# ScalarE's table sets named in the code: one set for Ln and Exp in each norm, the Silu set ahead of each feed-forward loop

## What is computed

```python
def rmsnorm(x, g):
    y = x * lax.rsqrt(jnp.mean(x * x, axis=-1, keepdims=True) + EPS)
    return y * g

def conv_ffn(h, w_gate, w_up, conv, w_down):
    u = dwconv3(h @ w_gate, conv)              # three taps along the tokens
    return (jax.nn.silu(u) * (h @ w_up)) @ w_down

for layer in range(DEPTH):
    mod = jax.nn.silu(cond) @ w_ada[layer] + b_ada[layer]
    shift1, scale1, gate1, shift2, scale2, gate2 = jnp.split(mod, 6)
    h = rmsnorm(x, norm_mix_g[layer]) * (1 + scale1) + shift1
    y = mixer_ab(h, ...) if layer % 2 == 0 else multiscale_pool(h, ...)
    x = x + gate1 * y
    h = rmsnorm(x, norm_ffn_g[layer]) * (1 + scale2) + shift2
    x = x + gate2 * conv_ffn(h, ...)
y = rmsnorm(x, final_norm_g)
```

## Time and profile before

| | |
|---|---|
| three runs | 1548.97, 1555.16, 1557.83 us |
| profiled execution | 1552.02 us, its span 1550.2 us |
| mean granted TensorE clock | 0.965 |
| TensorE matmul | 1417.5 us busy, 91% |
| VectorE | 1007.2 us, 65% |
| GpSimd | 670.3 us, 43% |
| ScalarE | 408.5 us, 26%, 50 table loads among its 718 instructions |
| DMA | 163.2 MB, mean 105 GB/s |

### The profile page before, as it was taken

How to read it: one execution, slowest core, us unless ns; L and a number is a source line. 1 busy time by engine, 2 the same in 40 slices (tenths; PEclk the granted TensorE clock), 3 DMA queues, 4 the chain that set the end, 5 groups by cost and what they waited for, 6 DMA issues and landing times.

```text
span 1550.2 us, 24701 instructions
## 1 busy us (share of the span) xinstructions
PE 1417.5 (91%) x9517; PEld 1376.2 (89%) x9517; DVE 1007.2 (65%) x1377; ACT 408.5 (26%) x718; POOL 670.3 (43%) x400
## 2 busy tenths in 40 slices
PE   3799979889979799999999999886999999999995
PEld 1598969888969699999999999875999999999995
DVE  4795688988666577787878887345664155325654
ACT  4723322155440633201110111256331011001122
POOL 0263544400515265565656554311454545454542
PEclk9899989999989899999999999987999999999998
DMA  9242312163123133443334442210332222222222
GB/s 380 101 136 96 100 37 69 55 227 116 50 71 122 68 122 135 171 148 135 122 116 169 144 140 76 74 41 14 122 108 82 68 82 68 71 78 81 66 72 79
DMA packets 44790, 163.23 MB, mean 105 GB/s; under 512 B 4800, under 2 KB 5952, under 8 KB 43584
## 3 DMA queue, kind: packets, MB, share of 16 engines
q1 hardware_dynamic: 44736, 162.52, 30.3%
HBM read 154.12 MB, written 6.82 MB: 104 GB/s over the span
## 4 chain that ended last, share of the span: by engine, by line
PE 69%; DVE 18%; issue 6%; ACT 5%; DMA 1%; ACTq 0%; POOL 0%; DVEq 0%; SPq 0%; POOLq 0%
PE ps L675 58%; DVE ada_raw L1454 3%; DVE work L1471 2%; DVE junk L1454 2%; DVE work L1477 2%; PE ps L960 2%; DVE work L1468 1%; ACT work L1029 1%; DVE blocks L1647 1%; PE ps L687 1%; DVE outer L1644 1%; DVE work L1847 1%; ACT work L1160 1%; ACT work L1360 1%; DVE qkv L1573 1%
## 5 line engine op out<-in xcount | busy, mean ns | idle before, releaser
L599 POOL TENSOR_SCALAR whi<-raw 128x1024 fp32r<-128x1024 f32 (+1 forms) x172 | 193.7, 1126 | 736.0 <-PE ps L675 567.8
L675 PE MATMUL ps<-hhi,whi 128*128 128x320 f32 x1984 | 461.5, 314 | 46.7 <-DVE hlo L1438 30.1
L675 PE MATMUL ps<-hlo,whi 128*128 128x320 f32 x1984 | 455.4, 311 | 0.0
L675 PE MATMUL ps<-hhi,wlo 128*128 128x320 f32 x1984 | 455.3, 311 | 0.0
L602 POOL TENSOR_TENSOR wlo<-raw,whi 128x1024 fp32r<-128x1024 f32 (+1 forms) x172 | 442.3, 2572 | 14.4
L675 PEld LDWEIGHTS ps<-hhi,whi 128*128 128x128 f32 x1984 | 335.4, 190 | 56.2 <-issue 32.6
L675 PEld LDWEIGHTS ps<-hlo,whi 128*128 128x128 f32 x1984 | 335.7, 190 | 0.0
L675 PEld LDWEIGHTS ps<-hhi,wlo 128*128 128x128 f32 x1984 | 335.3, 190 | 0.0
L675 PE MATMUL ps<-hidhi,whi 128*128 128x320 f32 x704 | 161.0, 310 | 2.8 <-DVE hidlo L1850 2.8
L675 PE MATMUL ps<-hidhi,wlo 128*128 128x320 f32 x704 | 161.0, 310 | 0.0
L675 PE MATMUL ps<-hidlo,whi 128*128 128x320 f32 x704 | 161.0, 310 | 0.0
(11 more groups left out here) (203 smaller groups left out, 1267.5 us busy)
## 6 DMA issues: line engine op xcount, KB each, us to landing
raw<-in_w_gu SPq DMA_DIRECT2D x88, 512.0 KB, 3.2
ada_raw<-in_w_rows SPq DMA_DIRECT2D x70, 512.0 KB, 3.5
raw<-in_w_in SPq DMA_DIRECT2D x28, 512.0 KB, 3.3
raw<-in_w_dn SPq DMA_DIRECT2D x32, 448.0 KB, 3.3
ada_first<-in_w_ada SPq DMA_DIRECT2D x4, 2048.0 KB, 21.6
raw<-in_w_dn SPq DMA_DIRECT2D x16, 512.0 KB, 3.3
row_late<-in_w_rows SPq DMA_DIRECT2D x10, 512.0 KB, 3.3
raw<-in_w_out SPq DMA_DIRECT2D x8, 512.0 KB, 4.1
```

The lines of the kernel that those rows point to most:

```text
L599: nc.gpsimd.tensor_scalar(whi[s][:, 0:n], raw[s][:, 0:n], 1.0, 0.0, ALU.mult, ALU.add).then_inc(s_whi, 1)
L675: last = nc.tensor.matmul(pair[pr][:, b], wt[s][:, cs], act[:, k, b * HALF:(b + 1) * HALF], start=(j == 0 and q == 0), stop=(j == len(tile ...
```

## The change

The warm-up Ln in `rsqrt_of_sums` and the one ahead of the scan output's norm are replaced by an explicit load of the set that holds both Ln and Exp. Ahead of the groups of each layer's feed-forward, behind the modulation, the Silu set is loaded by name. The activations, the waits and all other engines' streams stay as they are.

```diff
--- before.py
+++ after.py
@@ -45,6 +45,7 @@
 ADA_FFN = 48
 GROUPS = [8, 7, 7]
 EPS = 1e-6
+LN_EXP, SILU = "natural_log_exp_and_others", "silu_and_others"
 TILES = [S0 + P * t for t in range(SEQ_S // P)] + [P0]
 NT = len(TILES)
 BLOCK = 32
@@ -1006,7 +1007,7 @@
 
 
                 own.sync()
-                own.tick(nc.scalar.activation(warm[:], eps_col, ACT.Ln))
+                nc.scalar.preload_act_table_set(LN_EXP)
                 act.wait_ge(s_norm, q + 1)
                 if q:
                     act.wait_ge(s_a, 8 * q)
@@ -1292,8 +1293,7 @@
                 for n, (_, s_done) in enumerate(done_visits):
                     if s_done == s - 1:
                         o_squares(n)
-            own.sync()
-            own.tick(nc.scalar.activation(warm[:], eps_col, ACT.Ln))
+            nc.scalar.preload_act_table_set(LN_EXP)
             o_squares(NT - 1)
             own.sync()
             own.tick(nc.scalar.activation(ssq[:, 1], ssq[:, 0], ACT.Ln, bias=eps_col, scale=1.0 / DK))
@@ -1348,6 +1348,7 @@
                         mix_squares(g - 1)
                     mix_squares(3)
                     modulate(3, 1, 1)
+                nc.scalar.preload_act_table_set(SILU)
                 for g, nf in enumerate(GROUPS):
                     b = SEG["up", layer, g]
                     u, f = b["u"], b["f"]
```

## The result

The changed kernel takes 1539.39 us (median of six executions, 1538.80 to 1540.69). The kernel before, run six times beside it and earlier, takes 1552.18 us (1548.97 to 1557.83). The ratio is 0.992, 95% interval 0.9899 to 0.9942: 12.8 us, 0.8% faster. The forecast was 1541.6 us, range 1534 to 1550, with a gain of 12.0 us.

The account below looks back on a forecast made before the run. TensorE was taken to bound the kernel, with ScalarE and VectorE setting the time around the norms. Norms 7.7 plus layer 0's wait 2.8 and slow clock 1.5 made 12.0 us off 1553.6: 1541.6 us, range 1534 to 1550.

Parts of the forecast that it names:

- What bounds the kernel: Whole kernel: TensorE busy 91% of the span; a table load matters only where another engine ends up waiting for it.
- The norms, 7.7 us: Six norm places: one 1.28 us load between Ln and Exp goes at each, all on the path, 7.7 us gained.
- the upper bound: For one norm place: 1.4 us gained if the warm-up's share counts too.
- The Silu set ahead of the loops, 0 us: Ahead of each layer's feed-forward loops: one added 1.28 us load, hidden with about 1.1 us to spare, costs nothing.
- The loop loads of layer 1, 0 us: Layer 1's first feed-forward loop: VectorE has slack and TensorE never stops, so removing 16 loads gains nothing.
- The stall in layer 0, 4.3 us: End of layer 0's first feed-forward group: TensorE's 2.79 us wait for hidlo and 1.5 us of slow clock go.
- (a): Layer 0's stall stays or returns later through GpSimd, or some norms give half: gain 7.7 us, 1545.9; chance 0.14.
- (b): TensorE's clock no longer falls after the first norm (2.5 us) and in the mixer (2.4): gain 16.9, 1536.7; chance 0.10.
- They keep what they have: Layer 0's groups 1 and 2: their short waits for VectorE (three, 3.4 us together) stay unchanged.
- (e): Layer 0's groups 1 and 2: VectorE meets GpSimd in seven or more turns, 21.7 us lost, 1563; chance 0.04.
- (c): At the norms a switch costs more than its record, as if loaded twice: gain 19.7 us, 1533.9; chance 0.03.
- (d): At the norms Ln's own set is loaded again behind the wait, Exp load stays: 7.7 us slower, 1561.3; chance 0.04.

Follow-up runs that it names:

- e4: The changed kernel with two loads put between Ln and Exp at all six places, of which one was executed at each: 1550.56 us.
- e3: The changed kernel with the Silu set loaded ahead of layer 0's groups only, so layer 1's first loop keeps its 16 loads: 1538.42 us.
- e2: The kernel before with only the Silu set loaded ahead of the feed-forward groups of both layers, norms as before: 1549.91 us.
- e1: The norms-only kernel: the changed kernel without the Silu set ahead of the loops, one set for Ln and Exp kept: 1547.40 us.
- e11: The norms-only kernel (changed kernel without the Silu set ahead of the loops) run again unchanged, for its trace: 1548.82 us.
- e9: The changed kernel with one load put back, between Ln and Exp of the first norm only: 1542.49 us.
- e7: The changed kernel run once more, unchanged: 1539.95 us.
- e10: The kernel before run once more, unchanged, for its trace: 1552.80 us.
- e5: The changed kernel with a load ahead of unit A's copy in the eight turns of layer 0's first group, loop written out: 1539.24 us.
- e8: The changed kernel with the common Ln and Exp set used for the scan's q and k norms too, two loads fewer: 1537.61 us.
- e6: The changed kernel with a load ahead of Silu in the eight turns of layer 0's first group, loop written out: 1540.72 us.

## Why the prediction was right, and what it missed

**What bounds the kernel.** Right. ScalarE lost 47.5 us of busy time and the kernel 12.8; loads mattered only where they ended another engine's wait.

**The norms, 7.7 us.** Right in the mechanism and size: four waits of TensorE shrank by 1.28 or 1.29 us each, the last norm gave 1.40 (the upper bound named), e4 put four of the waits back to the hundredth. The drain of 1380 ns that the Trainium skill gives ("ScalarE: Activation LUTs", section "What ACT_TABLE_LOAD costs") isn't in these runs: taking a load away is worth its record of 1.28 us. The measurement decides. All six loads stood behind a wait for Ln to end, so what one costs right behind running work was not measured.

**The Silu set ahead of the loops, 0 us.** Right. The load of layer 0 begins right behind the last split; ScalarE then still waits 1.14 us for unit A (1.1 forecast):

```profile
526.76 1.28 ACT L1351 ACT_TABLE_LOAD   x1
529.18 0.70 ACT L1358 ACTIVATE work<-ps 128x640 f32<-128x640 f32 x1 [1.14 <-PE ps L676]
```

**The loop loads of layer 1, 0 us.** Right: e3.

**The stall in layer 0, 4.3 us.** Measured 4.6: the wait of 2.79 and 1.8 us of half clock instead of 1.5. The turn-by-turn reckoning holds to 0.3 us at its points. Counted from TensorE's last wait for hlo ahead of the loop (ended at 532.48 before, 527.03 after), turn 6's convolution was forecast at 87.3 and started at 87.37, turn 7's at 103.3 and started at 103.50, the end of hidlo at 112.3 came at 112.57:

```profile
614.40 0.74 DVE L1469 TENSOR_SCALAR work<-work,cols 128x640 f32<-128x640 f32 x1 [0.68 <-ACT work L1358]
...
630.53 2.68 DVE L1469 TENSOR_SCALAR work<-work,cols 128x640 f32<-128x640 f32 x1
...
638.78 0.82 DVE L1851 TENSOR_TENSOR hidlo<-work,hidhi 128x640 fp32r<-128x640 f32 x1 [0.90 <-ACT hidhi L1363]
```

TensorE would ask for it at 113.8, so the margin was 1.2 us and not 1.45. That the points came true so closely is in part luck. The reckoning kept each instruction's length of before, and single ones changed by 2 us: in turn 7 the first product takes 2.68 us instead of 0.54 and the last pair (L1478) 1.80 instead of 4.02; hidlo of turn 6 takes 2.60 instead of 0.83, the last row sum of that turn 2.06 instead of 3.41. Rival (a) named this stretching; the sums came out alike.

What the step did not see is that the stall has two sizes: with the norms changed and the loop loads left it is 5.95 us. The 4.3 us were read from the one trace of before and are right for the step from before to after and for the Silu set alone (4.6 in e2's trace), but too small for it on top of the norms (8.0 us by medians, 8.9 in the trace of e1, 10.1 in that of e11).

**The clock in the first stage.** This term was missing from the sum and stood under the rivals as half of (b), with 0.10 for both halves and 2.5 us for this one. It came (2.8 us, some 0.4 of it ahead of Ln) and it belongs to the change, as e9 and the table show. My argument against it compared 1.5 us of idle left with a fall after 2.79 elsewhere; that comparison spoke for it, not against, since the idle before the change was 2.77. The idle left is 2.02 us and not 1.5. The mixer's half did not come: its 48 products take 12.76 us after and 13.01 in e7, against 13.06.

**What hid the miss.** That 1541.6 lay so near 1539.39 is in part luck: -1.8 us from x arriving later and -1.5 us from waits in groups 1 and 2 happened to be about the size of the missing term. Neither is settled as chance. The sums start at 23.67 to 24.93 us in the three traces without the norms' half (before, e10, e2) and at 25.13 to 25.53 in all ten with it, though up to there the same instructions run and x, by its transfer, is what comes later. The waits vary within one kernel (3.4 and 2.0 us in the two traces of the kernel before), but the fourth one, 1.4 us in group 2, stands in six of the nine traces with the Silu set (4.8 to 5.0 us together; 3.5 in e5 and e8, 1.9 in e3) and in none of the four without. "They keep what they have" did not hold in after. Whether the change has a share in either is open.

**The rivals.** (a) and (e), VectorE held up by GpSimd, did not decide: VectorE is busy for 93.8 us in the loop's window against 86.4, and in layer 1 for 85.4 against 69.8, so it does meet GpSimd more often, and is on time all the same. (c) and (d) are out by the records. The range 1534 to 1550 held 1539.39.

## What to carry to other kernels

Look where the table loads lie in the trace, not how many there are: here 36 fewer loads save 46 us of ScalarE, of which 7.7 us lay on the path between Ln and Exp; the 16 in layer 0's loop brought 4.6 more through VectorE, the 16 in layer 1's nothing. A load inside a loop whose slow engine has spare time costs nothing singly, and two of them in a turn can push that engine past its slack; undo them together before judging one. Where TensorE waits a few microseconds for a short chain, a microsecond taken off that chain may also keep its clock at 2.4 GHz, so read the granted clock behind the wait in several traces before putting a price on it.

## What the runs showed of the hardware

- In the first stage TensorE's clock fell to 1.2 GHz behind idle stretches of 2.77 to 3.33 us (five traces) and stayed at 2.4 GHz behind 1.51 to 2.02 us (eight traces); with the fall the stage took 0.9 to 5.3 us more beyond the load itself.
- Two table loads of the same set next to each other left one record of 1283 ns (e4). A load of the set that is already loaded takes 1283 ns all the same (e4 and e9 between Ln and Exp, e5 and e6 in each turn). The gaps around a load between Ln and Exp are 0.01 to 0.02 us.
- A VectorE and a GpSimd instruction that overlapped did not share the delay: the one that started first took its usual time (1.22 us for VectorE's row sum, 1.04 for GpSimd's split), the second 2.06 and 2.11 us. This is one place in four traces (before and e10, e1 and e11).
- VectorE's busy time rose by 15.6 us in layer 1's first loop when 16 loads of ScalarE went, with the same instructions, and e3, which keeps these loads, has 69.4 us. Each turn the first product of the convolution is shorter (0.74 instead of 1.94 us), but the pair of instructions behind it (L1472) takes 3.0 instead of 1.0 and hidlo 2.6 instead of 1.4. In after a split of GpSimd (1063.94 to 1066.45 us) lies over that pair (1064.24 to 1067.26). TensorE lost nothing by it. A version without GpSimd's splits was not run.
- The stall at the end of layer 0's first group was 2.79 us in both traces of the kernel before and 5.95 and 5.93 us in both of norms-only. The traces part in the third turn, by 0.1 us against GpSimd. Where this 0.1 us comes from (in the first turn the load ahead of Silu already starts 0.28 us later) and how it grows to 3.2 us was not followed.
